# Fourteen gate strips of the first block computed by seven products behind the input norm instead of between the mixers' steps

## The reference

```
x = layer_norm(x, ln_in_w, ln_in_b)
z = x @ w_in[i]
z_ret, z_rwkv, z_gla, z_hgrn, z_gate = split_cols(z, GROUP_COLS)
branches = (retnet(z_ret), rwkv7(z_rwkv), gla(z_gla), hgrn2(z_hgrn))
for n in range(4):
    gate = sigmoid(z_gate[..., n * 1024:(n + 1) * 1024])
    merged = merged + gate * (branches[n] @ w_branch[i, n])
x = layer_norm(ALPHA * x + merged @ w_mix_out[i], ...)
```

## Time and profile before

| what | us |
|---|---|
| median of three runs (least to most) | 3287.34 (3284.38 to 3288.77) |
| the profiled execution, its own time | 3288.68 |
| its span | 3286.5 |
| PE busy | 3244.4 (99%) |
| DVE busy | 1872.9 (57%) |
| ACT busy | 1347.6 (41%) |
| POOL busy | 1352.3 (41%) |

### The profile page before, as it was taken

One profiled execution on the slowest core, in us unless ns is written; L12 is line 12 of the kernel. 1 busy time (PEld: TensorE's weight loads), 2 busy tenths in 40 slices (PEclk: granted clock), 3 DMA queues, 4 the chain that ended last, 5 costly groups with the idle time before them and its releaser, 6 DMA issues.

```text
span 3286.5 us, 48647 instructions
## 1 busy us (share of the span) xinstructions
PE 3244.4 (99%) x19042; PEld 2622.2 (80%) x19042; DVE 1872.9 (57%) x2504; ACT 1347.6 (41%) x2153; POOL 1352.3 (41%) x850
## 2 busy tenths in 40 slices
PE   9999999999999999999999999999999999999998
PEld 7877787777778878888788878888886888888886
DVE  6333425646446779777783446434663266555678
ACT  5333324343224464333443355224423353445444
POOL 4312124545322846544525654541112665454102
PEclk9999999999999999999999999999999999999999
DMA  4221213232537323333563344332343332345664
GB/s 129 75 65 59 69 56 114 79 100 72 147 93 247 114 80 101 97 106 100 200 200 100 94 120 123 103 117 87 114 133 108 121 96 80 120 157 196 217 194 148
DMA packets 413346, 388.83 MB, mean 118 GB/s; under 512 B 23584, under 2 KB 329632, under 8 KB 410304
## 3 DMA queue, kind: packets, MB, share of 16 engines
q1 hardware_dynamic: 386208, 341.68, 33.8%
q10 hardware_dynamic: 26912, 44.05, 3.9%
HBM read 295.58 MB, written 90.08 MB: 117 GB/s over the span
## 4 chain that ended last, share of the span: by engine, by line
PE 45%; DVE 3%; ACT 1%; issue 1%; POOL 0%; DMA 0%; DVEq 0%; ACTq 0%
PE psum L2152 18%; PE psum L5169 9%; PE psum L2792 8%; PE psum L3404 5%; PE psum L1737 2%; PE psum L1780 1%; PE psum L2828 1%; DVE ffn_form_lo L5158 0%; PE psum L1767 0%; DVE conv L3167 0%; DVE acc L5205 0%; ACT w_hi L2084 0%; PE psum L1755 0%; PE psum L1757 0%; DVE w_lo L2686 0%
## 5 line engine op out<-in xcount | busy, mean ns | idle before, releaser
L2103 POOL TENSOR_TENSOR w_lo<-w_raw,w_hi 128x1024 fp32r<-128x1024 f32 (+1 forms) x226 | 548.1, 2425 | 964.0 <-ACT w_hi L2084 962.0
L2084 ACT ACTIVATE w_hi<-w_raw 128x1024 fp32r<-128x1024 f32 (+1 forms) x227 | 234.6, 1034 | 396.2 <-PE psum L2152 338.9
L291 PE MATMUL psum<-x_hi,w_hi 128*128 128x512 f32 x832 | 355.0, 427 | 3.1 <-ACT gate L335 3.0
L291 PE MATMUL psum<-x_hi,w_lo 128*128 128x512 f32 x832 | 326.9, 393 | 0.0
L291 PE MATMUL psum<-x_lo,w_hi 128*128 128x512 f32 x832 | 326.4, 392 | 0.0
L2152 PE MATMUL psum<-x_hi,w_hi 128*128 128x512 f32 x816 | 312.6, 396 | 3.7 <-DVE w_lo L2112 1.9
L2152 PE MATMUL psum<-x_lo,w_hi 128*128 128x512 f32 x816 | 308.0, 390 | 0.0
L2152 PE MATMUL psum<-x_hi,w_lo 128*128 128x512 f32 x816 | 307.9, 390 | 0.0
L2686 POOL TENSOR_TENSOR w_lo<-w_raw,w_hi 128x512 fp32r<-128x512 f32 x117 | 159.0, 1360 | 127.5 <-ACT w_hi L2659 117.3
L291 PEld LDWEIGHTS psum<-x_hi,w_hi 128*128 128x128 f32 x832 | 156.8, 188 | 48.8 <-issue 14.9
L2152 PEld LDWEIGHTS psum<-x_hi,w_hi 128*128 128x128 f32 x816 | 153.2, 188 | 39.9 <-issue 5.1
(11 more groups left out here) (849 smaller groups left out, 7997.2 us busy)
## 6 DMA issues: line engine op xcount, KB each, us to landing
w_raw<-in_w_in SPq DMA_DIRECT2D x99, 512.0 KB, 4.5
merge_raw<-gates ACTq DMA_DIRECT2D x48, 512.0 KB, 4.7
x_raw<-mlp_forms SPq DMA_DIRECT2D x76, 256.0 KB, 3.4
gates<-gate SPq DMA_DIRECT2D x32, 512.0 KB, 3.0
w_raw<-in_w_mlp_out SPq DMA_DIRECT2D x54, 256.0 KB, 3.3
mlp_forms<-mlp_staged SPq DMA_DIRECT2D x13, 1024.0 KB, 3.9
w_raw<-in_w_ffn_up SPq DMA_DIRECT2D x24, 512.0 KB, 3.9
ffn_x_raw<-ffn_forms SPq DMA_DIRECT2D x46, 256.0 KB, 3.7
```

The source lines that it names most:

```text
L291: last = pe.matmul(bank, w[:, k, :], x[:, k, half(h)], start=(k == 0 and j == 0), stop=(k == KT - 1 and j == 2))
L2084: act.activation(self.view(self.c.wh, i), self.view(self.c.wr, i), ACT.Copy).then_inc(self.sig["w_hi"], 1)
L2103: pool.tensor_tensor(self.view(self.c.wl, i), self.view(self.c.wr, i), self.view(self.c.wh, i).bitcast(F32), ALU.subtract).then_inc(self.s ...
```

## The change

The gate strips 18 to 31 no longer stand between the mixers' steps. `first_group` makes them as seven pairs by `GateSevens`, on PE just ahead of the last rwkv strip (h = 1, j = 7; `HELD` is 15). The mixers keep the strips 0 to 17 (6, 3, 3 and 6 of them), and their tables are cut by 112 chunks in all. A new class `FirstForms` makes the forms of x between the strips of h = 1: POOL six wholes of 128x1024 and t1's lo, DVE one whole, four differences and three lo splits of 128x2048, ACT four hi splits of 128x2048. SP issues 28 loads of 256 KB for it ahead of the last strips' loads. `renew` gives used semaphores of the group a second name. ACT waits at the group's end until all results are stored. In the c steps' table c1, c3 and U have no chunk any more.

```diff
     def slot(self, sp, r):
-        if r >= 2:
+        if r >= self.own:
...
+class FirstForms:
...
+    def whole(self, eng, h, k, end):
+        eng.wait_ge(self.sig["x_lo"], KT * h + end)
+        return eng.tensor_tensor(self.x_in[:, k:end, half(h)], self.c.xh[:, k:end, half(h)].bitcast(F32),
+                                 self.c.xl[:, k:end, half(h)].bitcast(F32), ALU.add)
+    def whole_pool(self, pool, h, k):
+        self.whole(pool, h, k, k + 2).then_inc(self.sig["x_whole"], 1)
+    def sum(self, dve, i):
+        x11, x12, x22, x21 = (self.raw[n] for n in self.MADE)
+        if i == 0:
+            self.whole(dve, 1, KT // 2, KT).then_inc(self.sig["gate_t"], 1)
+            return
+        out, x, y = ((x11, x12, x11), (x12, x22, x12), (x22, x22, x11), (x21, x21, x22))[i - 1]
+        dve.wait_ge(self.sig["x_whole"], self.sig.at("x_whole", 6))
+        dve.wait_ge(self.sig["gate_t"], self.sig.at("gate_t", i))
+        dve.tensor_tensor(out, x, y, ALU.subtract).then_inc(self.sig["gate_t"], 1)
+    def hi(self, act, name):
+        act.wait_ge(self.sig["gate_t"], self.sig.at("gate_t", self.MADE.index(name) + 2))
+        act.activation(self.his[name], self.raw[name], ACT.Copy).then_inc(self.sig["gate_t_hi"], 1)
+    def low(self, eng, name, k, end):
+        eng.wait_ge(self.sig["gate_t_hi"], self.sig.at("gate_t_hi", self.MADE.index(name) + 1))
+        eng.wait_ge(self.sig["gate_t"], self.sig.at("gate_t", self.READ[name]))
+        return eng.tensor_tensor(self.los[name][:, k:end, :], self.raw[name][:, k:end, :],
+                                 self.his[name][:, k:end, :].bitcast(F32), ALU.subtract)
+    def lo(self, dve, name):
+        self.low(dve, name, 0, 4).then_inc(self.sig["gate_t_lo"], 1)
+    def lo_pool(self, pool, k):
+        self.low(pool, "t1", k, k + 2).then_inc(self.sig["gate_t1_lo"], 1)
...
+        def gates_by_sevens(n):
+            slots = [*(more_raw[:, i, :] for i in range(4)), *flat_place(core.wr, n - 1)]
+            places = [(more_w[:, 0, :], more_w[:, 1, :]), *zip(flat_place(core.wh, n - 2), flat_place(core.wl, n - 2)),
+                      *zip(flat_place(core.wh, n - 1), flat_place(core.wl, n - 1))]
+            feed = Feed(sig, slots, places, w_sums, Freed(st, sig, n, own=4))
+            forms = FirstForms(core, sig, raw, low, t_his)
+            x = {"b11": quarter(0, 0), "b21": quarter(4, 0), "b22": quarter(4, 1), **{t: forms.x(t) for t in FirstForms.MADE}}
+            sevens = GateSevens(core, st, sig, feed, forms, x, sum(p is not None for p in st.places), 0)
+            for i in range(gate_tiles[0], gate_tiles[1], 2):
+                sevens.plan(a["w_in"], GATE0 + i * P, gates, (i - KT) * P)
+            feed.elsewhere.update(range(1, sevens.count))
+            st.feeds.append(feed)
+            return feed, sevens, forms
...
-        for h, j in strips:
+        HELD = 2 * KT - 1
+        for n, (h, j) in enumerate(strips):
+            if n == HELD:
+                st.hold()
+                feed, sevens, forms = gates_by_sevens(st.held)
...
             norm.load(sp, a["x"], 1)
+            st.load(sp, 6)
+            feed.fetch(sp, 3)
+            st.load_held(sp)
+            feed.fetch(sp, len(feed.loads) - 1)
             st.load(sp, len(st.strips))
...
-            for h, j in strips:
+            for n, (h, j) in enumerate(strips):
                 t, i = tiles[h, j]
+                if n == HELD:
+                    for p in range(sevens.count):
+                        sevens.tensor(pe, p)
+                if n >= HELD:
+                    sevens.left(pe, n - HELD)
...
-            mixes(2 * KT - 8)
+            mixes(1)
+            forms.hi(act, "t1")
+            feed.hi(act, 0)
+            mixes(1)
+            forms.hi(act, "t3")
+            mixes(1)
+            forms.hi(act, "t2")
+            mixes(2)
+            forms.hi(act, "t4")
+            mixes(1)
+            for u in (1, 2):
+                feed.hi(act, u)
+            mixes(1)
+            for u in (3, 4):
+                feed.hi(act, u)
+            def resume(act, n):
+                if n in (4, 6):
+                    at = st.held + (n - 4) // 2
+                    st.hi(act, st.ends[at - 2], at + 1, True)
+            for p in range(sevens.count):
+                sevens.scalar(act, p, (lambda n: resume(act, n)) if p == sevens.count - 1 else None)
+            sevens.store(act, sevens.count - 1, "c12")
+            mixes(1)
+            sevens.all_stored(act)
...
-            shifts(2 * KT - 8)
+            forms.sum(dve, 0)
+            for i in range(1, 5):
+                forms.sum(dve, i)
+                shifts(1)
+            for name in FirstForms.SPLIT:
+                forms.lo(dve, name)
+                shifts(1)
+            for p in range(sevens.count):
+                sevens.vector(dve, p)
+            shifts(1)
...
-            for h, j in strips:
+            for n, (h, j) in enumerate(strips):
+                if n == HELD:
+                    for u in (3, 4):
+                        feed.lo(pool, u)
+                    for p in range(sevens.count):
+                        sevens.gpsimd(pool, p)
+                    for i in range(2):
+                        at = st.held + i
+                        st.lo(pool, st.ends[at - 2], at + 1, True)
                 st.lo(pool, tiles[h, j][0])
+                if 2 <= n < 8:
+                    forms.whole_pool(pool, *((0, 0), (0, 2), (0, 4), (0, 6), (1, 0), (1, 2))[n - 2])
+                if n == KT:
+                    feed.lo(pool, 0)
+                if n in (KT + 3, KT + 4):
+                    forms.lo_pool(pool, 2 * (n - KT - 3))
+                if n == KT + 5:
+                    for u in (1, 2):
+                        feed.lo(pool, u)
...
-    slot = first_group(nc, core, a, k, z, col_strip(w, HGRN0, 0), col_strip(w, HGRN0 + 512, 0))
+    slot = first_group(nc, core, a, k, z, gates, (18, 32), col_strip(w, HGRN0, 0), col_strip(w, HGRN0 + 512, 0))
...
-        gate_tiles(fill, range(12))
+        gate_tiles(fill, range(6))
...
-        gate_tiles(fill, range(12, 17))
+        gate_tiles(fill, range(6, 9))
...
-        gate_tiles(fill, range(17, 23))
+        gate_tiles(fill, range(9, 12))
...
-        gate_tiles(fill, range(23, 32))
+        gate_tiles(fill, range(12, 18))
...
-                            dict(norm=3, tr1=8, tr2=1, J2=1, J4=1, J8t=1, X4=1, X8=2, TW16=1, Y16=1, TW32=2, Y32=1, TW64=2,
-                                 Y64=1, TA=2, TAt=1, PP=1, c0=2, c1=1, c2=1, c3=1, U=1, y=1, bg=1),
-                            for_hgrn, (col(GLA0 + 512),), (col(GLA0),), [(zt[:, n, :], rows(z_hgrn, n)) for n in (2, 0, 4)], 15)
+                            dict(norm=2, tr1=5, tr2=1, J2=1, J4=1, J8t=1, X4=1, X8=1, TW16=1, Y16=1, TW32=1, Y32=1, TW64=2,
+                                 Y64=1, TA=1, TAt=1, PP=1, c0=1, c2=1, y=1, bg=1),
+                            for_hgrn, (col(GLA0 + 512),), (col(GLA0),), [(zt[:, n, :], rows(z_hgrn, n)) for n in (2, 0, 4)], 11)
...
-                              lambda n: dict(var=1, l0=12 if n == 0 else 5, l1=1, l2=1, l3=1, l4=1, l5=1, l6=1, l7=1, kt=3,
-                                             psi=2, y=3 if n == 0 else 2) | (dict(l0=3, kt=4, psi=3) if n == 2 else {}),
+                              lambda n: dict(var=1, l0=9 if n == 0 else 3, l1=1, l2=1, l3=1, l4=1, l5=1, l6=1, l7=1, kt=2,
+                                             psi=2, y=3 if n == 0 else 1) | (dict(l0=2, kt=3) if n == 2 else {}),
                               for_gla, (col(RET0),), (col(RET0 + P),),
...
-                               *between_rows(zt[:, 0:5:4, :], k["zero"])], 11)
+                               *between_rows(zt[:, 0:5:4, :], k["zero"])], 10)
...
-                              lambda n: dict(var=1, l0=9 if n == 0 else 5, l1=1, l2=1, l3=1, l4=1,
-                                             l5=1, l6=1, l7=1, kt=2 if n == 0 else 3, psi=2, y=3)
-                              | (dict(l0=3, kt=4, psi=3) if n == 1 else {}),
-                              for_ret, (col(GATE0 + 23 * P),), (col(GATE0 + 24 * P),),
+                              lambda n: dict(var=1, l0=5 if n == 0 else 3, l1=1, l2=1, l3=1, l4=1,
+                                             l5=1, l6=1, l7=1, kt=2, psi=1 if n == 0 else 2, y=1)
+                              | (dict(l0=2, kt=3) if n == 1 else {}),
+                              for_ret, (col(GATE0 + 12 * P),), (col(GATE0 + 13 * P),),
...
-                               *between_rows(zt[:, 1:6:4, :], k["zero"])], 11)
+                               *between_rows(zt[:, 1:6:4, :], k["zero"])], 9)
...
-                              lambda n: dict(score=3 if n == 0 else 2, kt=4, psi=2, y=2, var=3, mean=2), no_mixer,
-                              *((col_strip(a["w_branch"][1], c, 0, rows=2 * P, width=512), 2, P, 512) for c in (0, 512)), [], (0, 1, 3, 5, 9))
```

(2 more changed lines are left out.)

58 lines of the change are left out of this document (45 added, 13 removed).

## The result

The changed kernel takes 3346.78 us (median of 4 runs, 3345.72 to 3348.37) against 3287.45 for the kernel before beside it: ratio 1.0182, interval [1.0165, 1.02], 59.3 us **slower**. The forecast was 3317, range 3290 to 3336. The sign is right. The growth is twice the one forecast, and the time lies outside the range.

The account below looks back on a forecast made before the run. PE, busy 99% of the span, was taken to bound the kernel: 3288.7 - 19.1 (products) + 44.0 (new waits) + 5 (stage edges) = 3318.6, less 1.3 for the median of runs, 3317 us; range 3290 to 3336.

Parts of the forecast that it names:

- The priced waits: In the mixers, where chunks leave, PE newly waits for operands: six groups of places, 44.0 us in sum.
- y, 11 units: Ahead of y in hgrn's units 1 to 3, gla and ret: about 1.37 us wait each, 15.1 in all.
- norm and tr1: Rwkv's norm step and first transpose: 0.33 a unit, and 3.75 then 1.41 a unit; 9.3 us in all.
- hgrn's first level: First score level of hgrn: seven chunks taken, counted together against slack 4.92, leave a 4.6 us wait.
- gla's first level: First score level of gla: four chunks taken against a slack of 2.41 leave a 3.1 us wait.
- hgrn's last unit: First level in hgrn's last unit: two chunks taken against a slack of 0.49 leave a 2.2 us wait.
- the places priced at nothing: Other levels, rwkv's X8, TW32, TA, and ret's score, kt, psi, mean, var: slack taken to cover lost chunks; 0 us.
- the stage's edges: New stage behind the input norm: 2.5 us while forms are made, 2.5 at its end; +5 together (0 to 10).
- Rival B, the clock: New mixer waits slow PE's clock, 1.7 us each: 3322, or 3334 with some ten; forecast, B and C together 0.70.
- A: Mixers: DVE's chains shorten as POOL's lo splits leave; 3273 if every wait goes; chance 0.12.
- C: First group: DVE's forms hold the strips, edges +10 instead of +5, 3322; forecast, B and C together 0.70.
- D: Mixers: half the cover is not needed since waits don't add; half of the 44.0, 3295; chance 0.18.

Follow-up runs that it names:

- e7: The kernel before with 15 chunks of the linear mixers moved from ahead of y to kt or var, none removed; 3301.36 us, ratio 1.0044.
- e8: The kernel before with eight chunks per rwkv unit moved from norm, first transpose, c0, c1, c3 and U to ahead of bg; 3317.49 us, ratio 1.0095.
- e5: The changed kernel with POOL's and ACT's first-group work reordered and 12 strips moved, 16 chunks returned to rwkv's first transpose, c0, c1, c3; 3322.41 us, ratio 1.0107.
- e10: The kernel before with nine ret chunks moved from score, kt and psi in units 1 to 3 to ahead of var; 3287.82 us, ratio 1.0004.
- e4: The changed kernel with the first group reordered and eight strips moved instead of fourteen, 64 chunks leaving the mixers; 3302.64 us, ratio 1.0048 against before.
- e1: The changed kernel with ACT's and POOL's order changed in the first group only; 3337.05 us, ratio 1.0154 against before.
- e2: The changed kernel with only ACT's order changed in the first group, POOL's left as it was; 3347.63 us, ratio 1.0186 against before.
- e12: The kernel before with one chunk in ret's unit 0 moved from kt to psi; 3286.23 us, ratio 1.0.

## Why the prediction was right and wrong

**What bounds the kernel, and the products: right.** PE's time moved as PE's own work and waits said. The dense stage took 135.35 us for products of 133.9; block two's interval holds.

**The priced waits: right in sum, with luck in the parts.** The 44.0 measured 45.8 in after. Each figure is the growth of the distance between starts, good to some 0.5; at gla's first level the 3.4 us that before lost to the clock in the same stretch are taken out, since they count with the clock below.

| place | predicted | measured |
|---|---|---|
| y, 11 units | 15.1 | 14.1 |
| c0, c1, c3 | 9.7 | 9.2 |
| norm and tr1 | 9.3 | 11.9 |
| hgrn's first level | 4.6 | 5.0 |
| gla's first level | 3.1 | 5.6 |
| hgrn's last unit | 2.2 | 0 |

Three places are off by 2 us and more, and the misses cancel in part. At gla's first level PE idles 5.36 us: the slack of 2.41 was read where before's PE had been slowed by the clock; I read that delay as cover that the slack contained, which no run tests. Rwkv's first transpose waited 2.36 and 2.09 idle in units 1 and 2, where 1.41 was said. Hgrn's last unit didn't wait at all, for a reason given below. And at hgrn's start the 5.0 stand not at the level but at three gate chunks ahead of it (0.91, 0.28 and 2.93 idle); the last of them waits for the split that POOL makes right before the level's operands.

Two places in after as an example, y in hgrn, where DVE's update ends at 700.92 and PE follows 0.1 later, and a c step:

```profile
699.40 1.52 DVE L971 SCALAR_TENSOR_TENSOR hgrn_state<-hgrn_state,hgrn_end,hgrn_state_new 128x128 f32<-128x128 f32 x4
701.02 0.45 PE L689 MATMUL psum<-hgrn_qe,hgrn_state 128*64 128x128 f32 x4 [1.20 <-issue]
...
431.15 0.29 DVE L1598 TENSOR_TENSOR rwkv_state<-psum,rwkv_j2t 128x128 f32<-128x128 f32 x1 [1.30 <-PE psum L1332]
431.59 0.46 PE L1332 MATMUL psum<-rwkv_state,rwkv_j2t 128*128 128x128 f32 x2 [0.48 <-DVE rwkv_state L1598]
```

e7 and e8 reproduced the prices of y, c and the transposes in the kernel before, and e5 gave 22 us back for the sixteen chunks put where the price was.

**The step that failed first: the places priced at nothing.** The mixers lost 60.6 where 44.0 was said. Of the 14.8 beyond the priced places about 8 is the clock (below). The rest lies at places where the prediction found more slack than was taken: psi in ret (3.0), at and around kt in hgrn and gla (4.5; only 1.21 of it is PE waiting for kt's operand, most of the rest gate chunks waiting for ACT to empty a bank), and hgrn's second unit, whose first level and last two levels lost 4.9. In exchange the stall of the earlier trace rows went (2.2 gained), and many small places gave back some 4 in all. The error is one of method: I read a slack for each step, as if its producer's start were free. At psi the producer sits in DVE's queue behind other work that starts at a PE step further back, and every chunk between that step and this one hides the same time. I had used this reading for hgrn's first level, and there the size came out; not for psi and kt. For psi, e10 and e4 show it. For kt no run was made, so that there the cause stays open.

Hgrn's second unit shows a second thing that the prediction left out: with fewer gate strips, the splits of those that stay fall at other steps of POOL's queue. In after one stands right ahead of the first level's operands in the second unit, and PE waits there; in before one stood at the same place in the last unit, where the prediction read its slack of 0.49, and after has none there:

```profile
666.59 2.40 POOL L2107 TENSOR_TENSOR w_lo<-w_raw,w_hi 128x1024 fp32r<-128x1024 f32 x1 [13.01 <-ACT w_hi L2088]
671.44 1.11 PE L662 MATMUL psum<-hgrn_qe,hgrn_ke 64*64 64x64 f32 x16 [2.12 <-POOLq L1041]
...
635.30 2.39 POOL L2103 TENSOR_TENSOR w_lo<-w_raw,w_hi 128x1024 fp32r<-128x1024 f32 x1 [12.76 <-ACT w_hi L2084]
```

The first two lines are after's, the last is before's. So the 2.2 said for the last unit came in the second. This is read from the order of the queue; no run moved a split alone.

**The step that failed second: the stage's edges, +5 (0 to 10).** They cost 14.2: 12.7 in the first group and 1.45 at the end, where I had taken 2.5 each. I worked out DVE's time strip by strip, and the bound of 6 was for DVE's delays alone. I did not carry the three weight sums of the dense stage, which POOL runs, into POOL's queue, although the strip's split stands right behind them, nor the time that POOL and DVE take from each other. POOL's queue held the strip (e1 against e2), and the stall of 10.9 was followed by half clock.

**Rival B, the clock: right in kind, too small.** I gave three places at 1.7 each, up to ten. Six stretches came, 11.8 us before the credit of 3.4; the price of one is 1.7, gla's 3.4. What it takes was read from one stall of before at which the clock stayed full, and the slow stretch of before at 688 to 700 was left out. The Trainium skill, "TensorE: Matmul & The Clock Gate", section "HAM oscillation — how this bites in real kernels", says that idle stretches between bursts of matmuls let the gate fall back, and that each next burst pays; six places of the trace agree, and two don't: the idle 2.93 us ahead of 631.84 left the clock full, as did the shortest of rwkv's four (1.17). The stretch of before at 688 to 700 had no idle time ahead of it at all.

**Rivals A, C and D.** D (half of the cover isn't needed) falls: the priced waits came in full in their sum. A (chains shorten as splits leave POOL) acted at one place, hgrn's last unit, and the split came back in another unit; as a whole it falls too. C's edges, 10, were nearer to the 14.2 than mine. It named DVE's forms, which are in the chain, but with the same forms and another order of POOL's work the edges are 3.15 (e1).

## What to carry to other kernels

A piece of filler is priced not by the slack of the step that follows but from the PE step at which that operand's producer queue starts: all filler in between hides the same time, so take chunks in one account for the whole queue. Ask also where the helper work of the filler that stays (here POOL's splits) will stand afterwards. And a wait on the bound engine costs more than itself: filling the stalled engine even with useless work gave 6 us back here, since its clock stays up. Finally, a stage of denser work pays only where what it removes was not the cover of something else; here 19 us of products stood against 60 of lost cover.

## What the runs showed of the hardware

- **The clock falls behind short waits, and once without one.** The granted clock was 0.72 over 6 us, 1.7 us of work lost, behind idle times of PE of 2.09, 2.12, 2.36 and 3.85 us; 0.79 over 8 us behind 0.98 and 1.70 close together; and 0.50 over 6 us behind 5.36. It stayed at 1.00 behind 1.17 and 2.93. In before it was 0.72 from 688 to 700 with PE busy throughout, behind eight matmuls of 16x128 by 16x512; in e10 and e12, where this part of the kernel is the same, it was 0.83 over 10 us there (1.7 lost in place of 3.4). I had expected a fall at waits of 3 us and more. Length alone does not decide it; what else does was not tested.
- **DVE and POOL wait for each other's operations.** In the first group of after, a tensor_tensor of DVE and one of POOL that overlap end one behind the other, the later one its usual duration behind the earlier. DVE's usual 128x2048 takes 2.28 us (86.58, with POOL idle until near its end). Beside POOL a difference took 4.30 (81.62 to 85.92, behind POOL's split that ended at 83.77) and the whole form 4.03 (77.48 to 81.51, behind POOL's operation that ended at 79.37). POOL's sum of 128x512, usually 1.27, took 3.19 behind DVE's difference (ended 93.59), and the strip's split, usually 2.40, took 4.39 behind the next (ended 98.21). Even the shift's 128x1 operation (L3843), 0.15 us with POOL idle, took 1.22 until POOL's sum was done (94.73 and 94.71). So the 4.37 of a difference in the earlier trace rows is not its own time: the same operation takes 2.29 in two of its four places in block two of after. I had priced POOL's queue by the usual durations.
- **A hand-over is 0.10 to 0.15 us.** From the end of DVE's operation to the start of a waiting PE: 0.10 at y, 0.15 at the c step, 0.15 at psi. The 0.20 that I took from the earlier trace rows was no wait: PE's view of before shows no idle time at that step.
